# Longer runs from HBM, block turns on VectorE, and a down projection split by output columns in a streaming expert kernel

## The chip, the cores and the metric

The kernel runs on one core of one Trainium2 chip, the other cores idle. The metric is the device time of one execution in microseconds. Engines are named as in the profile: PE is TensorE (PEld its weight loads), DVE is VectorE, ACT is ScalarE, POOL is GpSimd, SP is SyncE, which here only issues DMAs.

## What is computed

One layer on 256 tokens of width 1024, all in float32: a mixer (input projection, two short convolutions, a gated recurrence, output projection), a layer norm, then an expert layer, and a second layer norm. The time goes to the expert layer. Cut to what matters:

```python
logits = xt @ w_router + b_router                 # 256 tokens, 32 experts
top_v, top_e = lax.top_k(logits, 4)
gates = softmax(top_v)
def expert(xb, e):                                # tokens routed to e
    h = xb @ w_gu[e] + b_gu[e]                    # 1024 -> 2048
    h_glu = min(h[:, :1024], 7); h_lin = clip(h[:, 1024:], -7, 7)
    act = h_glu * sigmoid(1.702 * h_glu) * (h_lin + 1)
    return act @ w_dn[e] + b_dn[e]                # 1024 -> 1024
ffn = sum over the 4 experts of a token of gate * expert(x)
x = layer_norm(DEEPNORM_ALPHA * x + ffn)
```

Each expert has 8.39 MB of gate-up weights and 4.19 MB of down weights, and all 32 are read once. On these inputs the reference routes between 21 and 44 tokens to an expert. The kernel handles them in blocks of 32 token slots: 18 experts take one block and 14 take two, 46 blocks in all. By expert number from 0, two blocks belong to 3, 4, 7 to 11, 14 to 16, 21, 24, 26 and 29.

## The kernel before, in words

**Loading.** SP issues all weight loads in one fixed order, on one queue. `gu_buf` holds two experts' gate-up weights, by the parity of the expert, each in four chunks of 2 MB (`GC` = 4, two slices `k` of 128 input rows each). `dn_buf` holds one expert's down weights in two halves of 2 MB (`DC` = 2). In the streaming loop (L270 to L274) the order is: down of expert e, then gate-up of expert e+1. A gate-up chunk may be overwritten when the last block of the expert two before has used it (`gu_used`), a down half when the last block of the expert before has used it (`dn_used`). Partition p of a gate-up chunk holds rows p and 128+p of the chunk's 256 rows, so one partition's part is two runs of 8 KB; of a down half it is four runs of 4 KB. One exception in the order stands at the start: the second down half of expert 2 (L266) and the load of `b_dn` (L268) come before the gate-up weights of expert 3.

**One block on PE** (`expert_block`, L790). PE multiplies 32 token slots by weights 256 or 512 columns at a time, and puts four such products side by side in the array, one in each group of 32 array columns, writing 32 of the 128 PSUM partitions each. Every float32 matmul is two instructions. In order: the gate-up product into bank `HB` (L797), its bias by a one-hot product (L807), the gather of the next block's 32 tokens (L757, `gather`), the first half of the sum of the *previous* block's results into the token accumulators (`combine(0)`, L767), two 128x128 transposes of the activation (`turn(TB, lin)`, L763), `combine(1)`, transposes of the gated one-hot (`gated`, which becomes `back`, the matrix that sends slots to tokens) and of the gathered rows, and the down product (L834). The down product leaves, for a group j of 256 hidden units, a partial sum over all 1024 output columns on partitions 32j to 32j+31, in banks `Y0` and `Y1`; `combine` adds the four partial sums in the same 128-row product that sends slots to tokens. The accumulators fill banks 0 to 3 for the whole expert loop.

**The other engines in a block.** DVE makes `gated` and the next `onehot`, clamps, multiplies to the activation `lin` (L619 to L625), copies the turned activation out of PSUM (L628) and half of the result (L630). ACT does the sigmoid, copies `rows`, `back`, `rows_t` and the other half of the result (L386 to L394).

**Start and end.** `start_sum` (L710) puts the scaled input in the accumulators, between the router's steps. At the end PE does one last `combine`, and DVE computes the layer norm's statistics of each 512-column piece as soon as it is summed (L634), then normalises, and SP stores.

## Time and profile before

| | us |
|---|---|
| median of 3 runs (lowest, highest) | 1086.83 (1084.99, 1091.21) |
| span of the profiled execution | 1088.8 |
| PE busy, share of the span | 946.0 (87%) |
| PE weight loads | 367.4 (34%) |
| DVE busy | 249.4 (23%) |
| ACT busy | 112.2 (10%) |
| moved by DMA | 422.59 MB, mean 388 GB/s over the span |
| chain that ended last, by engine | PE 63%, DMA 26%, SP's queue 8% |

A busy share is a mean over stages with different limits: the stage before about 125 us is the mixer and the router, then comes the expert stream, and from about 1063 us the end. The profiled execution lies 2.0 us above the median of the runs. Stretches are given in microseconds from the start of the span. The landing of a transfer is read from the instruction that waited for it.

### The profile page before, as it was taken

The numbers are of one execution on the slowest core, as the hardware profiler recorded it, in microseconds if no ns is written. First come the engines' busy times: TensorE is split into PE (matmuls) and PEld (weight loads), VectorE is DVE, ScalarE is ACT, GpSimd is POOL, SyncE is SP. The second block draws the span as 40 slices with busy tenths as digits, with TensorE's granted clock in tenths as the row PEclk, the third lists the DMA queues.
The fourth block names the chain that finished last, engine by engine and source line by source line (L and its number), as shares of the span: only waits on it lengthen the run. The fifth ranks groups of instructions, "written<-read, shape, count | busy, mean of one in ns | idle before, by whom it ended". The sixth has DMA issues, their size and how long they took to land.

```text
span 1088.8 us, 16845 instructions
## 1 busy us (share of the span) xinstructions
PE 946.0 (87%) x6739; PEld 367.4 (34%) x6740; DVE 249.4 (23%) x661; ACT 112.2 (10%) x265; POOL 7.3 (1%) x26
## 2 busy tenths in 40 slices
PE   8999998999669999997699997666977897976986
PEld 7884432333113333331133332211322332321322
DVE  3552511222112222221022221111211221211214
ACT  1300210111001111110011110000100110100100
POOL 1000000000000000000000000000000000000000
PEclk9999999999979999998899998888998998987998
DMA  9978689999999999999999999999999999999995
GB/s 328 410 281 337 252 353 396 418 388 372 417 418 388 381 416 372 376 372 417 419 406 417 380 373 417 417 417 419 418 419 418 417 412 417 392 417 417 396 420 224
DMA packets 80135, 422.59 MB, mean 388 GB/s; under 512 B 5804, under 2 KB 8152, under 8 KB 47352
## 3 DMA queue, kind: packets, MB, share of 16 engines
q1 hardware_dynamic: 77848, 421.96, 95.8%
q10 hardware_dynamic: 2272, 0.41, 0.2%
q8 instruction: 12, 0.20, 0.1%
q14 instruction: 3, 0.02, 0.0%
HBM read 421.30 MB, written 1.05 MB: 388 GB/s over the span
## 4 chain that ended last, share of the span: by engine, by line
PE 63%; DMA 26%; SPq 8%; issue 1%; DVE 1%; ACT 0%; DVEq 0%
DMA gu_buf<-in_w_gate_up_dram 21%; PE ps L797 20%; PE ps L767 12%; PE ps L834 12%; SPq L249 7%; PE ps L667 6%; DMA dn_buf<-in_w_down_dram 5%; PE ps L807 3%; PE ps L757 3%; PE ps L695 3%; PE ps L763 2%; SPq L254 1%; DMA gu_buf<-in_w_in_dram 0%; PE ps L682 0%; SPq L243 0%
## 5 line engine op out<-in xcount | busy, mean ns | idle before, releaser
L797 PE MATMUL ps<-gu_buf,rows_t 128*32 128x512 f32 x2944 | 379.5, 659 | 127.4 <-DMA gu_buf<-in_w_gate_up_dram 125.4
L797 PEld LDWEIGHTS ps<-gu_buf,rows_t 128*32 128x32 f32 x2944 | 95.3, 116 | 394.6 <-issue 202.7
L767 PE MATMUL ps<-mix,back 128*128 128x512 f32 x376 | 181.5, 606 | 0.0
L834 PE MATMUL ps<-dn_buf,act_t 128*32 128x512 f32 x1456 | 166.3, 595 | 1.3 <-DMA dn_buf<-in_w_down_dram 1.3
L619 DVE TENSOR_SCALAR glu<-ps 128x256 f32<-128x256 f32 x46 | 19.5, 425 | 404.2 <-PE ps L807 404.2
L630 DVE COPY mix<-ps 128x512 f32<-128x512 f32 x46 | 31.8, 692 | 247.2 <-PE ps L834 247.2
L767 PEld LDWEIGHTS ps<-mix,back 128*128 128x128 f32 x376 | 64.0, 190 | 65.2 <-issue 64.4
L386 ACT ACTIVATE sig<-glu 128x256 f32<-128x256 f32 x46 | 19.1, 416 | 576.5 <-DVE glu L619 576.5
L834 PEld LDWEIGHTS ps<-dn_buf,act_t 128*32 128x32 f32 x1456 | 42.4, 109 | 91.8 <-issue 73.9
L667 PE MATMUL ps<-turned,gu_buf 128*128 128x256 f32 x320 | 69.6, 379 | 1.3 <-DMA gu_buf<-in_w_in_dram 1.3
L667 PEld LDWEIGHTS ps<-turned,gu_buf 128*128 128x128 f32 x320 | 60.6, 190 | 9.7 <-issue 1.5
L807 PE MATMUL ps<-turned,bias_sel 128*32 128x512 f32 x368 | 52.4, 633 | 0.0
L757 PE MATMUL ps<-xs,onehot 128*32 128x256 f32 x752 | 50.5, 382 | 0.0
L757 PEld LDWEIGHTS ps<-xs,onehot 128*32 128x32 f32 x752 | 25.3, 112 | 38.7 <-issue 30.3
L394 ACT COPY mix<-ps 128x512 f32<-128x512 f32 x46 | 27.0, 586 | 108.4 <-PE ps L834 108.4
L390 ACT COPY back<-ps 128x256 f32<-128x256 f32 x46 | 17.1, 373 | 168.7 <-PE ps L763 168.7
L614 DVE TENSOR_SCALAR gated<-onehot,gates 128x128 f32<-128x128 f32 x92 | 22.2, 283 | 53.2 <-issue 53.2
L628 DVE COPY act_t<-ps 128x256 f32<-128x256 f32 x46 | 19.5, 425 | 53.5 <-PE ps L763 53.5
L605 DVE TENSOR_SCALAR onehot<-slot_iota,block_base,places 128x128 f32<-128x128 f32 x92 | 27.7, 344 | 7.2 <-DVE gated L614 7.2
L695 PE MATMUL ps<-gu_buf,mix 128*128 128x512 f32 x64 | 27.6, 592 | 0.0
L807 PEld LDWEIGHTS ps<-turned,bias_sel 128*32 128x32 f32 x368 | 13.9, 125 | 35.4 <-issue 35.4
L763 PEld LDWEIGHTS ps<-ident,gated 128*128 128x128 f32 x92 | 13.0, 142 | 24.2 <-issue 24.2
(173 smaller groups left out, 346.4 us busy)
## 6 DMA issues: line engine op xcount, KB each, us to landing
gu_buf<-in_w_gate_up_dram SPq DMA_DIRECT2D x128, 2048.0 KB, 24.1
dn_buf<-in_w_down_dram SPq DMA_DIRECT2D x63, 2048.0 KB, 16.3
gu_buf<-in_w_in_dram SPq DMA_DIRECT2D x4, 2048.0 KB, 17.1
gu_buf<-in_w_out_dram SPq DMA_DIRECT2D x2, 2048.0 KB, 14.4
gu_buf<-in_w_in_dram SPq DMA_DIRECT2D x2, 1024.0 KB, 6.6
xs<-in_x_dram SPq DMA_DIRECT2D x2, 512.0 KB, 3.6
late<-in_ln_g_dram SPq DMA_DIRECT2D x2, 512.0 KB, 21.6
late<-in_ln_b_dram SPq DMA_DIRECT2D x2, 512.0 KB, 18.3
```

The costliest lines, as they stand in the source:

```text
L249: sp.dma_start(gu_buf[:, b, GK * c:GK * (c + 1), :], gu_src[bass.ds(e, 1)].rearrange("o p k n -> p (o k) n")[:, GK * c:GK * (c + 1), :]).t ...
L394: nc.scalar.copy(y_sb[:, 0:512], ps[:, Y0, :]).then_inc(S["y0_sb"], 1)
L605: ins = V.tensor_scalar(onehot[:, h], slot_iota[:], base, column(h), ALU.add, ALU.is_equal)
L630: V.tensor_copy(y_sb[:, 512:D], ps[:, Y1, :]).then_inc(S["y1_sb"], 1)
L667: ins = T.matmul(half(banks[c // 2], c % 2), w_piece[:, piece_slot[i], k, P * c:P * (c + 1)], turned[:, k, :], start=(k == 0), stop=(k == ...
L695: return T.matmul(ps[:, 2 * h + c, :], mix[:, k, P * h:P * (h + 1)], w_out_v[:, n, 512 * c:512 * c + 512], start=(n == 0), stop=(n == KT - 1))
L757: ins = T.matmul(ps[SLOTS * j:SLOTS * (j + 1), Y0, 0:QF], onehot[:, h, 0, :], xs[:, h, QF * j:QF * (j + 1)], start=(h == 0), stop=(h == TH ...
L763: ins = T.transpose(ps[:, bank, P * b:P * (b + 1)], src[:, P * b:P * (b + 1)], ident[:])
L767: return [T.matmul(ps[:, 2 * h + c, :], back[:, P * h:P * (h + 1)], y_sb[:, 512 * c:512 * c + 512], start=False, stop=False, skip_group_ch ...
L797: ins = T.matmul(ps[SLOTS * j:SLOTS * (j + 1), HB, :], rows_t[:, k % 2, SLOTS * (k // 2):SLOTS * (k // 2 + 1)], gu_buf[:, b, k, :].rearran ...
L807: ins = T.matmul(ps[SLOTS * j:SLOTS * (j + 1), HB, :], bias_sel[:, j, :], b_gu, start=False, stop=True)
L834: ins = T.matmul(ps[SLOTS * j:SLOTS * (j + 1), Y0 + c, :], act_t[:, m, SLOTS * j:SLOTS * (j + 1)], weights[j][:, 512 * c:512 * c + 512], s ...
```

## The change

- **Runs.** Partition p now holds rows 8p to 8p+7 of a weight matrix. A chunk of gate-up or a half of down is one run of 16 KB per partition, and one partition's runs lie 64 KB (gate-up) or 32 KB (down) from the next one's. What is loaded, its chunks and their order stay, but `b_dn` is now loaded in four pieces before the expert loop.
- **Turns.** With rows 8p+q on partition p, the 32x32 block transpose of DVE gives the stationary operand that slice q needs. `rows_t` and `act_t` are each made by one DVE instruction that reads the source with a step of 8 elements; PE's transposes of `lin` and `rows`, and four copies (three on ACT, one on DVE; one of them L630), go.
- **Down by output columns.** Group j now computes output columns 256j to 256j+255 over all 1024 hidden units: 32 matmuls of 256 columns in place of 16 of 512, into half of one bank. `combine` is four products per token half, each of 32 rows (the slots of one group) by 256 columns, each with its own group of array rows and its own accumulator bank j. Both halves run in one place, after the gather; the gate-weighted `b_down` goes the same way.
- **Bias first.** The bias product opens the accumulation in `HB` in place of closing it, so the last gate-up chunk releases the result.
- **Start and end.** `start_sum` moves into the first expert block, in the place of its `combine`. The end has eight statistics of 256 columns, all after the last sum.

```diff
-        gu_src = w_gate_up[0].rearrange("e (k p) n -> e p k n", p=P)
-        dn_src = w_down[0].rearrange("e (j m p) n -> e m p j n", p=P, m=DC)
+        gu_src = w_gate_up[0].rearrange("e (p k) n -> e p (k n)", p=P)
+        dn_src = w_down[0].rearrange("e (p q) n -> e p (q n)", p=P)
...
+            for j in range(GROUPS):
+                sp.dma_start(b_dn[E * j:E * (j + 1), :], b_down[0][:, QF * j:QF * (j + 1)]).then_inc(S["bdn_in"], 16)
             sp.wait_ge(S["bounds_ok"], 1)
...
-            sp.dma_start(b_dn, b_down[0]).then_inc(S["bdn_in"], 16)
...
                 nc.scalar.activation(sig[:], glu[:], ACT.Sigmoid, scale=SWIGLU_ALPHA).then_inc(S["sig_ok"], 1)
-                act.wait_ge(S["rows_ps"], now)
-                nc.scalar.copy(rows[:], half(Y0, 0)).then_inc(S["rows_sb"], 1)
                 act.wait_ge(S["back_ps"], now)
-                nc.scalar.copy(back[:], half(Y1, 0)).then_inc(S["back_sb"], 1)
-                act.wait_ge(S["rows_t_ps"], now)
-                nc.scalar.copy(rows_t[:], half(HB, 0).rearrange("p (b s) -> p b s", b=2)).then_inc(S["rows_t_ok"], 1)
-                act.wait_ge(S["y0_ps"], now)
-                nc.scalar.copy(y_sb[:, 0:512], ps[:, Y0, :]).then_inc(S["y0_sb"], 1)
+                nc.scalar.copy(back[:], half(TB, 0)).then_inc(S["back_sb"], 1)
+                act.wait_ge(S["y_ps"], now)
+                nc.scalar.copy(y_sb, half(YB, 0)).then_inc(S["y_sb"], 1)
...
+            def in_blocks(v):
+                return v.rearrange("p (a q) -> p q a", q=KT)
...
+            dve.wait_ge(S["rows0_ps"], 1)
+            V.transpose(rows_t[:], in_blocks(half(Y0, 0))).then_inc(S["rows_t_ok"], 1)
...
+                dve.wait_ge(S["act_ok"], now)
+                V.transpose(act_t[:], in_blocks(lin[:])).then_inc(S["act_t_sb"], 1)
+                dve.wait_ge(S["rows_ps"], now)
+                V.transpose(rows_t[:], in_blocks(half(RB, 0))).then_inc(S["rows_t_ok"], 1)
...
-                dve.wait_ge(S["y_ps"], now)
-                V.tensor_copy(y_sb[:, 512:D], ps[:, Y1, :]).then_inc(S["y1_sb"], 1)
+                dve.wait_ge(S["back_ps"], now)
...
-            def combine(c):
-                return [T.matmul(ps[:, 2 * h + c, :], back[:, P * h:P * (h + 1)], y_sb[:, 512 * c:512 * c + 512],
-                                 start=False, stop=False, skip_group_check=True) for h in range(TH)]
+            def combine(h, stationary, moving):
+                for j in range(GROUPS):
+                    ins = T.matmul(ps[:, j, QF * h:QF * (h + 1)], stationary[SLOTS * j:SLOTS * (j + 1), P * h:P * (h + 1)],
+                                   moving[SLOTS * j:SLOTS * (j + 1), :], start=False, stop=False, skip_group_check=True)
+                return ins
...
+                pe.wait_ge(S["sel_bias"], now)
+                for j in range(GROUPS):
+                    T.matmul(ps[SLOTS * j:SLOTS * (j + 1), HB, :], bias_sel[:, j, :], b_gu, start=True, stop=False)
                 pe.wait_ge(S["rows_t_ok"], now)
...
-                                           start=(k == 0), stop=False)
+                                           start=False, stop=(k == KT - 1))
...
-                            ins = T.matmul(ps[SLOTS * j:SLOTS * (j + 1), Y0 + c, :], act_t[:, m, SLOTS * j:SLOTS * (j + 1)],
-                                           weights[j][:, 512 * c:512 * c + 512], start=(m == 0), stop=(m == DC - 1))
+                            ins = T.matmul(ps[SLOTS * j:SLOTS * (j + 1), YB, 0:QF], act_t[:, DK * m + q, :],
+                                           weights[q][:, QF * j:QF * (j + 1)],
+                                           start=(m == 0 and q == 0), stop=(m == DC - 1 and q == DK - 1))
```

On PE, the body of one block in the loop over pairs of experts, before (x4 and the like count matmuls of a run; `ps` is PSUM, `mix` there holds the result copied out of PSUM, `turned` the bias table):

```order
L797 MATMUL ps<-gu_buf,rows_t 32x512 x32
L807 MATMUL ps<-turned,bias_sel 32x512 x4
L757 MATMUL ps<-xs,onehot 32x256 x8
L767 MATMUL ps<-mix,back 128x512 x2
L763 MATMUL ps<-ident,lin 128x128 x2
L767 MATMUL ps<-mix,back 128x512 x2
L763 MATMUL ps<-ident,gated 128x128 x2
L763 MATMUL ps<-ident,rows 128x128 x2
```

and of the changed kernel, the same body with its down product:

```order
L809 MATMUL ps<-turned,bias_sel 32x512 x4
L812 ISA
L815 MATMUL ps<-gu_buf,rows_t 32x512 x32
L773 MATMUL ps<-xs,onehot 32x256 x8
L785 MATMUL ps<-mix,back 128x256 x8
L779 MATMUL ps<-ident,gated 128x128 x2
L840 REGISTER_ALU
L843 MATMUL ps<-dn_buf,act_t 32x256 x16
L840 REGISTER_ALU
L843 MATMUL ps<-dn_buf,act_t 32x256 x16
```

The bias moved ahead of the gate-up product, the two halves of `combine` stand together as eight short products, and between the gate-up product and the down product four transposes are gone.

On DVE, the part of the block's body after the gate-up product, before:

```order
L619 TENSOR_SCALAR glu<-ps 128x256
L620 TENSOR_SCALAR lin<-ps 128x256
L622 SCALAR_TENSOR_TENSOR lin<-lin,glu 128x256
L625 TENSOR_TENSOR lin<-lin,sig 128x256
L626 REGISTER_ALU
L626 COPY bias_sel<-ident 128x128
L628 COPY act_t<-ps 128x256
L630 COPY mix<-ps 128x512
```

and in the changed kernel:

```order
L635 TENSOR_SCALAR glu<-ps 128x256
L636 TENSOR_SCALAR lin<-ps 128x256
L638 SCALAR_TENSOR_TENSOR lin<-lin,glu 128x256
L641 TENSOR_TENSOR lin<-lin,sig 128x256
L643 STREAM_TRANSPOSE act_t<-lin 128x256
L645 STREAM_TRANSPOSE rows_t<-ps 128x256
L646 REGISTER_ALU
L646 COPY bias_sel<-ident 128x128
```

The turn of the activation follows the last multiply directly, without PE between them, and the copy of the result has left DVE.

## Rows read from the trace of the kernel before

**Rows 1.** The page: GB/s in 40 slices, and the gate-up group.
```profile
GB/s 328 410 281 337 252 353 396 418 388 372 417 418 388 381 416 372 376 372 417 419 406 417 380 373 417 417 417 419 418 419 418 417 412 417 392 417 417 396 420 224
...
L797 PE MATMUL ps<-gu_buf,rows_t 128*32 128x512 f32 x2944 | 379.5, 659 | 127.4 <-DMA gu_buf<-in_w_gate_up_dram 125.4
```
**Rows 2.** Windows: stretch, length, busy of five engines, PE clock, DMA share, GB/s.
```profile
271.00:316.00 45.00, 27.25 (x186) 7.05 (x182) 5.72 (x16) 2.01 (x5) 0.00 (x0) 0.88 1.01 418
411.00:444.00 33.00, 33.00 (x276) 11.91 (x272) 7.89 (x22) 4.02 (x10) 0.00 (x0) 1.00 0.94 381
```
**Rows 3.** Chain of waits, one PE-bound block: start, us, engine and line.
```profile
205.34 6.87 PE ps L797 x64
212.21 0.86 PE ps L807 x8
213.07 0.86 PE ps L757 x16
213.93 1.91 PE ps L767 x4
215.84 0.22 PE ps L763 x2
216.06 1.72 PE ps L767 x4
217.78 0.44 PE ps L763 x4
218.22 3.57 PE ps L834 x32
```
**Rows 4.** Timeline of PE: start, duration, group, and the wait before it.
```profile
505.21 1.92 PE L797 MATMUL ps<-gu_buf,rows_t 128*32 128x512 f32 x16 [1.66 <-DMA gu_buf<-in_w_gate_up_dram]
510.19 3.45 PE L797 MATMUL ps<-gu_buf,rows_t 128*32 128x512 f32 x16 [3.06 <-DMA gu_buf<-in_w_gate_up_dram]
...
514.33 1.04 PE L757 MATMUL ps<-xs,onehot 128*32 128x256 f32 x16
...
525.39 1.06 PE L797 MATMUL ps<-gu_buf,rows_t 128*32 128x512 f32 x8 [2.16 <-DMA gu_buf<-in_w_gate_up_dram]
```
**Rows 5.** Windows, the mixer's stretch with runs of 2 KB.
```profile
15.00:24.00 9.00, 9.00 (x44) 7.89 (x43) 4.80 (x29) 1.80 (x4) 0.00 (x0) 1.00 1.10 363
```
**Rows 6.** Groups by line: duration per instruction after the bar.
```profile
L390 ACT COPY back<-ps 128x256 f32<-128x256 f32 x46 | 17.1, 373 | 168.7 <-PE ps L763 168.7
...
L873 PE MATMUL ps<-mix,turned 32*128 32x512 f32 x8 | 3.7, 600 | 0.0
```
**Rows 7.** Timeline of DVE in one block.
```profile
514.58 0.42 DVE L619 TENSOR_SCALAR glu<-ps 128x256 f32<-128x256 f32 x1 [16.33 <-PE ps L807]
...
515.83 0.42 DVE L625 TENSOR_TENSOR lin<-lin,sig 128x256 f32<-128x256 f32 x1
...
517.54 0.42 DVE L628 COPY act_t<-ps 128x256 f32<-128x256 f32 x1 [1.14 <-PE ps L763]
```
**Rows 8.** The page, DMA issues: count, KB each, median us from issue to landing.
```profile
gu_buf<-in_w_gate_up_dram SPq DMA_DIRECT2D x128, 2048.0 KB, 24.1
dn_buf<-in_w_down_dram SPq DMA_DIRECT2D x63, 2048.0 KB, 16.3
...
xs<-in_x_dram SPq DMA_DIRECT2D x2, 512.0 KB, 3.6
```
**Rows 9.** Timeline: SP's first streamed loads.
```profile
126.96 6.84 SPq L249 DMA_DIRECT2D gu_buf<-in_w_gate_up_dram  x4
```
**Rows 10.** Timeline: the last block and the end.
```profile
1062.93 3.57 PE L797 MATMUL ps<-gu_buf,rows_t 128*32 128x512 f32 x16 [3.06 <-DMA gu_buf<-in_w_gate_up_dram]
1066.32 1.03 PE L807 MATMUL ps<-turned,bias_sel 128*32 128x512 f32 x8
...
1078.89 0.70 DVE L498 BATCH_NORM_STATS2 small<-ps 128x6 f32<-128x512 f32 x1 [0.16 <-PE ps L767]
...
1084.92 1.40 DVE L515 SCALAR_TENSOR_TENSOR xs<-ps,small,late 128x512 f32<-128x512 f32 x2
```

More of the change, by code:

```diff
@@ L786, in turn_gates, with expert_block @@
                 for h in range(TH):
-                    ins = T.transpose(ps[0:E, TB, P * h:P * (h + 1)], gates[:, h, :], ident[:])
+                    for j in range(GROUPS):
+                        ins = T.matmul(ps[E * j:E * (j + 1), TB, P * h:P * (h + 1)], gates[:, h, :], ident[:], start=True, stop=True)
                 ins.then_inc(S["gates_t_ps"], 1)
-            def expert_block(now, after, b, loads, down, first=False):
+            def expert_block(prior, now, b, loads, down, first=False):
+                pe.wait_ge(S["sel_bias"], now)
+                for j in range(GROUPS):
+                    T.matmul(ps[SLOTS * j:SLOTS * (j + 1), HB, :], bias_sel[:, j, :], b_gu, start=True, stop=False)
                 pe.wait_ge(S["rows_t_ok"], now)
@@ L848, in expert @@
                 with pe.Fori(first, end) as g:
-                    expert_block(g + 1, g + 2, b, loads, down)
+                    expert_block(g, g + 1, b, loads, down)
             down_0 = [down_at(m, 16) for m in range(DC)]
-            expert_block(1, 2, 0, 16, down_0, first=True)
+            expert_block(0, 1, 0, 16, down_0, first=True)
             pe.wait_ge(S["bounds_ok"], 1)
@@ L867, in _ @@
                 pair_of_experts(pair)
-            pe.wait_ge(S["bdn_in"], 16)
+            pe.wait_ge(S["bdn_in"], 16 * GROUPS)
             pe.wait_ge(S["gates_t_ok"], 1)
             for h in range(TH):
-                for c in range(2):
-                    T.matmul(ps[:, 2 * h + c, :], gates_t[:, P * h:P * (h + 1)], b_dn[:, 512 * c:512 * c + 512],
-                             start=False, stop=False, skip_group_check=True)
+                combine(h, gates_t, b_dn)
             with pe.Fori(E // 2 - 1, E // 2) as pair:
```

175 lines of the change are left out of this document (80 added, 95 removed).

## Prediction

> **What bounds the kernel now.** I read the page's GB/s line first. It has a ceiling: from the seventh slice on it stands at 416 to 420 in 19 of 33 slices and dips to between 372 and 412 in the others [rows 1]. The windows say what the two kinds are. From 271 to 316 us PE is busy 27 of 45 us and waits, and 418 GB/s arrive; from 411 to 444 PE is busy throughout and only 381 arrive [rows 2]. So the stream has two regimes: where experts have one block, the transfers bind, and where two-block experts follow each other, PE does. An expert is 12.58 MB, 30.1 us at 418 GB/s; the chain of waits gives a block 6.87+0.86+0.86+1.91+0.22+1.72+0.44+3.57 = 16.45 us of PE without a gap [rows 3], so two blocks take 32.9 us. SP's loads are released by PE's use, so each such expert leaves the queue dry for about 2.8 us. The page counts 2944 gate-up matmul instructions, 64 to a block, 46 blocks [rows 1].
>
> How much is lost so? In the timeline the third and fourth gate-up chunks of one expert land at 505.21 and 510.19, 4.98 us apart; the next landing PE waited for, 525.39, comes after two down halves and a chunk, 15.20 us, so a down half takes 5.11 us [rows 4]. Of the 128 gate-up chunks 8 are loaded before the stream, of the 63 down halves 2 before it and 2 after the last chunk [rows 8]: 120 and 59 lie between the first issue at 126.96 [rows 9] and the last landing at 1062.93 [rows 10]. With a full queue they take 120 x 4.98 + 59 x 5.11 = 899 us; they take 936. After about 2 us of latency (a 512 KB load takes 3.6, of which 1.3 is data [rows 8]) some **35 us** are queue idle. PE's slack in the one-block stretches is worth nothing.
>
> **The change, part by part.**
>
> *PE's block.* Bias, gate-up product and gather keep their shapes: 0.86 + 6.87 + 0.86. The down product streams as many columns, 32 matmuls of 256 for 16 of 512. Its shape (32 output rows, 256 columns) is the gather's, whose 8 matmuls take 0.86 in the chain [rows 3]; four times that is 3.4, and I keep 3.57. The transposes of `lin` and `rows` go, 0.22 each. `combine` was 1.91 + 1.72. Eight products of 32 rows by 256 columns now: no row shows four row groups at once. The nearest for a low bound is the gather, where four column groups share the array, 0.86 for the same count; the high bound is one after another: an instruction of 512 columns takes 1.72/4 = 0.43 in a stream [rows 3], and 16 of half the columns 3.4 (few rows make none shorter: those of the `b_down` product on 32 rows are listed at 0.60 like the others [rows 6]). I take 1.1, nearer the gather, since each row group has its own accumulator bank.
>
> The Trainium skill (TensorE: Matmul & The Clock Gate, Part 3: Packing small matmuls) gives four row tiles 3.07 times the speed of one after another; no run so far shows it here. By that the combine is 3.4/3.07 = 1.1 us.
>
> *The turn takes the lead.* PE cannot start the down product before `act_t`. In one block the gather starts at 514.33 [rows 4], the clamp on DVE at 514.58, and the last multiply ends at 516.25 [rows 7]. A block turn of 128x256 is not in the trace. Its low bound is nothing saved or lost against the copy out of PSUM, 0.42 [rows 7]; as a high one I take the four copies' worth, 1.7, for a read with a step of 8. I choose 0.42, the row of the same size and type. Then `act_t` is ready 1.67 + 0.03 + 0.42 after the clamp starts, 2.4 after the gather, and PE starts the down product at 2.5. PE's own work there is 0.86 + 1.1 + 0.22 = 2.2, so it waits 0.3: the combine is hidden as long as it costs less than 1.4. Behind the wait on PE stands only the down product. The turn of the rows comes next on DVE, 0.42 more, and is needed only when the next gate-up product starts, 4 us later; the one-hot copy behind it too is early. ACT loses three copies, DVE one; neither engine was late. **A block is 0.86 + 6.87 + 2.5 + 3.57 = 13.8 us**, two are 27.6.
>
> *Runs.* A down half in runs of 4 KB is 32 runs per DMA engine, a gate-up chunk in runs of 8 KB is 16, for the same bytes: 5.11 - 4.98 = 0.13 us for 16 runs more, 8 to 9 ns each [rows 4]. Runs of 2 KB arrived at only 363 GB/s [rows 5], in the same sense. With 8 runs of 16 KB, both kinds take 4.98 - 8 x 0.009 = **4.90 us** (428 GB/s), an estimate from those landings. An expert is 29.4 us, above two blocks at 27.6: PE is never late in the stream. The bounds: no gain over 8 KB runs, 4.98 (or over today's mean, 5.02); the layout's wide steps could cost, see the rivals.
>
> *Does the queue stay full?* For a two-block expert whose last chunk lands at t, its down halves land by t + 9.8 and the next expert's chunks by t + 29.4. The first block ends at about t + 11.6, the second at t + 25.4, so the next down half is issued at t + 23.6, 5.8 us before the queue is dry. At the start, the second down half of expert 2 no longer waits for a slow pair of blocks: PE comes to it some 4 us earlier, and 1 or 2 us of idle may stay there. The first block's `combine` becomes `start_sum`, 8 full products, 3.4 us as by the high bound above, which is what the old combine cost there. The bias ahead of the first gate-up product delays its first chunk, and SP's first issue, by about 0.3 us; the four `b_dn` loads fall in a stretch in which SP waits for the block bounds.
>
> *The end.* Before, from the last chunk's landing 15.96 us pass to the last sum (1078.89), and 9.9 from there to the end of the span [rows 10]. Now: 3.4 us for that chunk as before, when the bias started 3.39 after the landing (16 instructions take 3.45 and 3.57 after waits of 3.06, and 1.92 after one of 1.66) [rows 4, 10]; the bias, 0.86, is ahead; `act_t` 2.5 later; half of the down product, then a wait for the last down half, which lands at 9.8 (two transfers); 1.8 for the other half, 0.25 and a copy of 0.37 like ACT's of the same size [rows 6], 1.1 for the sums: 13.3, so 2.6 less. But all statistics now follow the last sum: eight of 256 columns at about 0.42 are 3.4, for two of 0.70 that followed it before [rows 10]: 2.0 more. The end is 25.9 - 0.6 = 25.3 us.
>
> **Sum.** 127.3 + 2 + 179 x 4.90 = 1006.4 for the last chunk's landing, + 25.3 = 1031.7 of span. The span of the profiled execution was 2.0 above the median of the runs, so **1029.7 us**. Of the 57 us, 35 are idle of the queue that goes, 22 the longer runs, less 0.3, and 0.6 comes at the end.
>
> **Rivals.**
>
> *A: the longer runs bring nothing.* The queue is always full but moves at today's mean of 5.02 (the DMA engines' share of 1.01 to 1.02 in full stretches [rows 2] says they have no gaps to give back). 129.3 + 899 + 25.3 - 2 = 1052 us. For it: no 16 KB run is in the trace. Against: two run lengths differ by a steady cost for each run.
>
> *B: PE still binds.* The four row groups run one after another, or the turn takes over 1.3 us. Serial: 0.86 + 3.4 + 0.22 + 0.1, a block of 15.9, two are 31.8 against 29.4: 2.4 of idle per two-block expert where it was 2.8, about 30 us in all: 1060. It decides from a block of 14.7 us. Against: column groups do run together [rows 3].
>
> *C: the wide steps between runs slow HBM, and the kernel is slower than before.* [...] The point from which the change loses is (1088.8 - 25.3 - 129.3)/179 = 5.22 us a transfer, 402 GB/s: 4% below today's rate in full stretches is enough. At 380 GB/s (5.52) the time is 1141. For it: nothing in this trace has such steps. Against: nothing either, beyond that the old layout had steps of 1 MB between the runs of one partition, at 418.
>
> The Trainium skill (DMA: Bandwidth & Descriptors, Latency and other measured facts) has a rule that speaks for C: tiles of 16 KB rows lose rate at large power-of-two pitches, from 2 MB on to 164 of 214 GB/s, while 512 KB still gave 207. The pitch here is 64 KB, so by its figures at most a few per cent are lost; no row here shows it.
>
> **How the numbers follow.** Forecast 0.62, A 0.17, B 0.11, C 0.08, and 0.02 for something in the first or last stage. The range must hold 8 in 10: forecast and A, with B's lower part. Below, runs at no cost each would be 4.98 - 16 x 0.009 = 4.84, 1019; above, B ends at 1060. So 1018 to 1060. About 0.5% is what a measurement of this kernel can tell from no change. Forecast, A and B are all faster by more; of C a third is near the old time. Faster 0.90, same 0.03, slower 0.07.
>
> **What would show it.** The GB/s line should be flat at 425 or more from 130 us to the end; A shows 418 flat, B dips, C lies flat and low. Landings should be 4.90 apart in both kinds. A block should last 13.8 in a two-block expert, PE's wait ahead of the down product should be for DVE's turn (0.3), with the turn at 0.42, and PE should wait for gate-up chunks in every expert. The first streamed load should be at about 127, the last chunk's landing at 1006. I am wrong in kind if the rate falls under 402 GB/s, or if PE shows no waits for chunks.

## The result, and the profile after

The changed kernel takes 1043.35 us, the median of 4 runs (1041.63 to 1045.26), against 1087.49 us (4 runs, 1084.99 to 1091.21) for the kernel before: a ratio of 0.9588, with a 95% interval of 0.9555 to 0.962. The forecast was 1029.7, so the time lies in its range, 13.6 us above the forecast itself. The profiled execution took 1045.26 us, with a span of 1043.3.

The page of the changed kernel: busy time and instructions of the engines, the granted clock and GB/s in 40 slices, and the groups of the two products (duration of one after the bar).

```profile
PE 834.9 (80%) x8423; PEld 361.2 (35%) x8424; DVE 242.2 (23%) x666; ACT 72.6 (7%) x171; POOL 6.1 (1%) x23
...
PEclk9999989899888999998899998877998998988987
...
GB/s 326 412 326 311 218 430 329 427 420 422 428 431 408 423 416 432 427 428 430 427 429 429 427 430 426 430 428 428 430 428 427 431 427 428 417 428 431 427 427 207
...
L815 PE MATMUL ps<-gu_buf,rows_t 128*32 128x512 f32 x2944 | 377.8, 658 | 117.5 <-DMA gu_buf<-in_w_gate_up_dram 117.5
...
L843 PE MATMUL ps<-dn_buf,act_t 128*32 128x256 f32 x2912 | 177.1, 389 | 50.6 <-DMA dn_buf<-in_w_down_dram 42.9
```

Beside [rows 1] the GB/s line is higher (427 to 432 where it was 416 to 420) and nearly flat, where it dipped in 14 of 33 slices. It is not quite flat: the seventh slice shows 329, the thirteenth 408, and a few others 416 to 423. Windows of the two stretches of [rows 2], which are 430 and 427 GB/s now instead of 418 and 381:

```profile
271.00:316.00 45.00, 29.76 (x280) 9.29 (x272) 7.29 (x22) 1.95 (x5) 0.00 (x0) 0.86 1.01 430
411.00:444.00 33.00, 31.43 (x384) 12.79 (x380) 7.55 (x22) 2.70 (x7) 0.00 (x0) 1.00 1.00 427
```

The timeline of PE in an expert with one block, and then a block of an expert with two, beside [rows 3, 4]; in brackets the wait before a group and what ended it:

```profile
507.54 1.92 PE L815 MATMUL ps<-gu_buf,rows_t 128*32 128x512 f32 x16 [2.98 <-DMA gu_buf<-in_w_gate_up_dram]
512.43 3.59 PE L815 MATMUL ps<-gu_buf,rows_t 128*32 128x512 f32 x16 [2.97 <-DMA gu_buf<-in_w_gate_up_dram]
517.34 1.92 PE L815 MATMUL ps<-gu_buf,rows_t 128*32 128x512 f32 x16 [1.32 <-DMA gu_buf<-in_w_gate_up_dram]
...
522.23 1.93 PE L843 MATMUL ps<-dn_buf,act_t 128*32 128x256 f32 x32 [0.66 <-DMA dn_buf<-in_w_down_dram]
527.13 1.93 PE L843 MATMUL ps<-dn_buf,act_t 128*32 128x256 f32 x32 [2.97 <-DMA dn_buf<-in_w_down_dram]
```

```profile
338.48 1.06 PE L809 MATMUL ps<-turned,bias_sel 128*32 128x512 f32 x8 [0.92 <-issue]
339.35 7.05 PE L815 MATMUL ps<-gu_buf,rows_t 128*32 128x512 f32 x64
346.22 1.05 PE L773 MATMUL ps<-xs,onehot 128*32 128x256 f32 x16
347.20 1.15 PE L785 MATMUL ps<-mix,back 32*128 32x256 f32 x16
348.28 0.44 PE L779 MATMUL ps<-ident,gated 128*128 128x128 f32 x2
348.96 3.42 PE L843 MATMUL ps<-dn_buf,act_t 128*32 128x256 f32 x57 [0.24 <-DVE act_t L643]
```

Chunks land 4.89 to 4.91 us apart and the two down halves 4.90, where it was 4.98 and 5.11. In the block of the second fence PE starts its down product 2.74 us after the gather. Of what had been `combine` and transposes (1.91, 0.22, 1.72, 0.44 in [rows 3]) there remain one `combine` of 1.08 us from start to start and the transposes of `gated`.

The last block and the end, beside [rows 10]:

```profile
1018.33 3.23 PE L815 MATMUL ps<-gu_buf,rows_t 128*32 128x512 f32 x16 [1.96 <-DMA gu_buf<-in_w_gate_up_dram]
...
1024.05 1.93 PE L843 MATMUL ps<-dn_buf,act_t 128*32 128x256 f32 x32 [0.18 <-DVE act_t L643]
1028.12 1.93 PE L843 MATMUL ps<-dn_buf,act_t 128*32 128x256 f32 x32 [2.13 <-DMA dn_buf<-in_w_down_dram]
1030.54 1.15 PE L785 MATMUL ps<-mix,back 32*128 32x256 f32 x16 [0.49 <-ACT mix L401]
```

The last chunk lands at 1018.33 instead of 1062.93, 44.6 us earlier, and the span ends 25.0 us later, where it was 25.9. So all but 1 us of the 45.5 us of span is gained in the stream. The sum of the prediction put that landing at 1006.4. The first streamed load is issued at 127.23 as it said (127.3), so the 11.9 us are lost in between, and the page says where to look first: the seventh slice. PE and windows of the DMA there:

```profile
137.66 3.42 PE L843 MATMUL ps<-dn_buf,act_t 128*32 128x256 f32 x60
146.30 1.93 PE L809 MATMUL ps<-turned,bias_sel 128*32 128x512 f32 x8 [5.22 <-issue]
148.00 8.35 PE L815 MATMUL ps<-gu_buf,rows_t 128*32 128x512 f32 x64
```

```profile
156.00:159.00 3.00, 2.82 (x42) 1.45 (x38) 2.47 (x6) 0.72 (x2) 0.00 (x0) 1.00 0.69 289
159.00:162.00 3.00, 3.00 (x60) 1.80 (x56) 1.31 (x6) 0.07 (x1) 0.00 (x0) 1.00 0.03 11
162.00:165.00 3.00, 2.35 (x32) 0.69 (x27) 0.00 (x0) 0.37 (x1) 0.00 (x0) 1.00 0.51 147
```

Between the only block of expert 0 and the first of expert 1, PE stands still for 5.22 us with nothing to wait for ("issue"). After that its bias product runs at half speed (1.93 instead of 1.07). SP is behind that block: it waits to load the second down half of expert 2 and cannot go on to the chunks of expert 3, and for some 5 us next to nothing is moved.

### The profile page after: what moved, and what is told of

The parts are those of the page before. It is cut to its first block, busy times and chain, and to the rows that moved or that the text cites. A ratio compares the mean times of both kernels' runs of the same rounds, so it can differ in the third digit from the quotient of the medians.

```text
span 1043.3 us, 20077 instructions
## 1 busy us (share of the span) xinstructions
PE 834.9 (80%) x8423; PEld 361.2 (35%) x8424; DVE 242.2 (23%) x666; ACT 72.6 (7%) x171; POOL 6.1 (1%) x23
## 4 chain that ended last, share of the span: by engine, by line
DMA 51%; PE 40%; DVE 6%; issue 2%; SPq 0%; ACT 0%; DVEq 0%; POOL 0%; POOLq 0%
DMA dn_buf<-in_w_down_dram 51%; PE ps L815 14%; PE ps L843 13%; PE ps L683 7%; PE ps L711 3%; PE ps L809 2%; DVE act_t L643 1%; DVE lin L641 1%; DVE lin L638 1%; DVE glu L635 1%; DVE lin L636 1%; PE ps L666 0%; PE ps L698 0%; PE ps L730 0%; PE ps L671 0%
## 5 line engine op out<-in xcount | busy, mean ns | idle before, releaser
L843 PE MATMUL ps<-dn_buf,act_t 128*32 128x256 f32 x2912 | 177.1, 389 | 50.6 <-DMA dn_buf<-in_w_down_dram 42.9
L843 PEld LDWEIGHTS ps<-dn_buf,act_t 128*32 128x32 f32 x2912 | 90.1, 111 | 123.5 <-DMA dn_buf<-in_w_down_dram 56.9
L809 PE MATMUL ps<-turned,bias_sel 128*32 128x512 f32 x368 | 54.7, 668 | 22.4 <-issue 22.4
L773 PE MATMUL ps<-xs,onehot 128*32 128x256 f32 x752 | 53.3, 404 | 0.0
L785 PE MATMUL ps<-mix,back 32*128 32x256 f32 x736 | 52.7, 400 | 0.5 <-ACT mix L401 0.5
L785 PEld LDWEIGHTS ps<-mix,back 32*128 32x128 f32 x736 | 33.2, 184 | 21.3 <-issue 19.3
L630 DVE TENSOR_SCALAR gated<-onehot,gates 128x128 f32<-128x128 f32 x92 | 22.2, 284 | 66.9 <-issue 66.9
L401 ACT COPY mix<-ps 128x256 f32<-128x256 f32 x46 | 17.1, 372 | 213.2 <-PE ps L843 213.2
L643 DVE STREAM_TRANSPOSE act_t<-lin 128x256 f32<-128x256 f32 x46 | 29.7, 645 | 1.6
L711 PE MATMUL ps<-gu_buf,mix 128*128 128x512 f32 x64 | 27.6, 592 | 0.0
L809 PEld LDWEIGHTS ps<-turned,bias_sel 128*32 128x32 f32 x368 | 9.6, 115 | 41.0 <-issue 39.0
L779 PE MATMUL ps<-ident,gated 128*128 128x128 f32 x92 | 20.1, 300 | 0.0
L641 DVE TENSOR_TENSOR lin<-lin,sig 128x256 f32<-128x256 f32 x46 | 19.6, 425 | 1.6
## 6 DMA issues: line engine op xcount, KB each, us to landing
late<-in_ln_g_dram SPq DMA_DIRECT2D x2, 512.0 KB, 23.5
```

The costliest lines, as they stand in the source:

```text
L630: ins = V.tensor_scalar(gated[:, h, :], onehot[:, h].rearrange("p j s -> p (j s)"), gates[:, h, bass.ds(e, 1)], None, ALU.mult)
L641: V.tensor_tensor(lin[:], lin[:], sig[:], ALU.mult).then_inc(S["act_ok"], 1)
L643: V.transpose(act_t[:], in_blocks(lin[:])).then_inc(S["act_t_sb"], 1)
L711: return T.matmul(ps[:, 2 * h + c, :], mix[:, k, P * h:P * (h + 1)], w_out_v[:, n, 512 * c:512 * c + 512], start=(n == 0), stop=(n == KT - 1))
L773: ins = T.matmul(ps[SLOTS * j:SLOTS * (j + 1), Y0, 0:QF], onehot[:, h, 0, :], xs[:, h, QF * j:QF * (j + 1)], start=(h == 0), stop=(h == TH ...
L785: ins = T.matmul(ps[:, j, QF * h:QF * (h + 1)], stationary[SLOTS * j:SLOTS * (j + 1), P * h:P * (h + 1)], moving[SLOTS * j:SLOTS * (j + 1) ...
```

## Experiments

### The two halves of the change apart

`before_long` is the kernel before with the new layout of the weights in HBM read (runs of 16 KB). `after_short` is the changed kernel with the old runs, 8 KB for gate-up and 4 KB for down. In both the weights are multiplied with the rows in another pairing; the work is the same.

```diff
# before_long, against the kernel before
-        gu_src = w_gate_up[0].rearrange("e (k p) n -> e p k n", p=P)
-        dn_src = w_down[0].rearrange("e (j m p) n -> e m p j n", p=P, m=DC)
+        gu_src = w_gate_up[0].rearrange("e (p k) n -> e p (k n)", p=P)
+        dn_src = w_down[0].rearrange("e (p q) n -> e p (q n)", p=P)
# after_short, against the changed kernel
-        gu_src = w_gate_up[0].rearrange("e (p k) n -> e p (k n)", p=P)
-        dn_src = w_down[0].rearrange("e (p q) n -> e p (q n)", p=P)
+        gu_src = w_gate_up[0].rearrange("e (c k p) n -> e c p k n", p=P, c=GC)
+        dn_src = w_down[0].rearrange("e (j m p) n -> e m p j n", p=P, m=DC)
```

> The kernel before with the loads of the changed one: one run of 16 KB per partition, the block on PE as it was. The rows of the weights reach the wrong slices, so the output is not the reference's; every instruction and byte is. Theory (transfers of 4.90 us, but the pairs of blocks of 32.9 us on PE stay as they are): only the 18 one-block experts can gain their 0.73 us, about 13 us, 1075, with the PE-bound stretches still at 381 GB/s. Rival (the rate gives its 22 us wherever it acts, since the queue is what ends last): 1066. If long runs bring nothing without the other parts: 1088.

> The changed kernel with the old run lengths, two runs of 8 KB for a gate-up chunk and four of 4 KB for a down half; output not the reference's, since the rows of the weights reach the wrong slices. Theory: transfers of 4.98 and 5.11 again, 22 us more, less some idle that longer transfers cover (up to 5 us): 1060 to 1065. Rival on the 5.2 us for which PE stood still after its first block (an instruction fetch held up by long runs on the same DMA engines): that stall shrinks to the 1.4 of the kernel before and the time is 4 us lower still; if the jump causes it, it stays at 5.

Measured: `before_long` 1073.78 us (1072.2 to 1075.17), ratio 0.9866 (0.9843 to 0.9889); `after_short` 1064.37 us (1063.44 to 1064.41), ratio 0.9784 (0.9763 to 0.9805). The GB/s lines of the two:

```profile
GB/s 326 415 293 342 224 385 387 427 384 372 430 429 400 382 420 371 372 371 430 429 430 427 374 373 430 427 429 429 407 430 429 429 410 429 417 430 430 385 430 218
```

```profile
GB/s 326 409 310 309 236 416 332 418 415 416 417 417 420 419 418 417 417 418 417 417 418 419 418 418 417 418 417 417 418 419 419 417 417 417 416 418 416 419 418 225
```

The first has the new ceiling (427 to 430) and the old dips (371 to 387): where PE binds, longer runs bring nothing. The second has the old ceiling (415 to 420) and no dips but the one in the seventh slice. The layout alone saves 14.1 us and the PE side alone 23.5; together 44.1 to 44.5, so 7 us come only when both are there: a faster stream is worth more once PE no longer binds. In `after_short` the stop of PE is still there, 5.57 us long, so it does not come from the layout.

### What about the runs is it: their length or their distance

The prediction's rival C made the distance between the runs of neighbouring partitions the danger. `after_close` reads runs of 16 KB that lie side by side; `after_short_wide` reads the old run lengths at distances of 64 and 32 KB. The pairing of weights and rows is another in both, the work the same.

```diff
# after_close
-        gu_src = w_gate_up[0].rearrange("e (p k) n -> e p (k n)", p=P)
+        gu_src = w_gate_up[0].rearrange("e (c p k) n -> e c p (k n)", p=P, c=GC)
# after_short_wide
+        gu_src = w_gate_up[0].rearrange("e (p k c) n -> e c p k n", p=P, c=GC)
```

> The changed kernel with runs of 16 KB that lie next to each other: partition p of a 2 MB transfer takes the p-th 16 KB of one contiguous 2 MB, in place of runs 64 KB (32 KB for down) apart; output not the reference's, since the rows of the weights reach the wrong slices. Theory (only the length of a run counts): landings 4.90 apart as in the changed kernel, 1043. Rival C of the prediction (wide steps cost something): faster landings and over 5 us less; 4.85 a transfer would be 1034.

> The changed kernel with runs of 8 KB and 4 KB, but with the partitions as far apart as in it (64 KB and 32 KB); output not the reference's, for the same reason. Theory: as the run with short runs in the old places, 1064, transfers of 4.98 and 5.11. Rival (wide steps cost, and long runs hide it): slower than 1064 by over 5 us.

Measured: `after_close` 1043.57 us (1040.56 to 1046.08), 0.9571 (0.9538 to 0.9605), landings 4.88 to 4.90 apart (500.72, 505.61, 510.51, 515.39); `after_short_wide` 1064.59 us (1064.0 to 1067.46), 0.9781 (0.9748 to 0.9814), landings 4.97 and 5.12. Each is the time of its partner with the other distance, so of the two only the length of a run counts here, at these distances, and C is false.

### Where 12 us of the stream went

`after_noif` leaves out PE's loop for further blocks of expert 0, which has only one block with these inputs; it is thus no kernel for all inputs. `after_order` keeps everything and lets SP issue the first two chunks of expert 3 ahead of the second down half of expert 2.

```diff
# after_noif
             pe.wait_ge(S["bounds_ok"], 1)
-            end = pe.value_load(bounds[0:1, 1:2], min_val=1, max_val=MAXB)
-            with pe.If(end > 1):
-                with pe.Fori(1, end) as g:
-                    expert_block(g, g + 1, 0, 16, down_0)
# after_order
-            stream_dn_chunk(2, 1, blocks_before(2))
-            stream_gu(3, 1)
+            used = blocks_before(2)
+            for c in range(GC):
+                sp.wait_ge(gu_used[c], used)
+                sp.dma_start(gu_chunk(1, c), gu_src[3][:, GRUN * c:GRUN * (c + 1)]).then_inc(gu_in[1][c], 16)
+                if c == 1:
+                    stream_dn_chunk(2, 1, used)
```

> The changed kernel without the loop for further blocks of expert 0, which has one block on these inputs (the general case is left out). Theory (the jump over that loop's code makes PE fetch instructions, 5.2 us, and with it comes a dry queue at 158 to 163 us): PE goes on at about 142, the dry spell nearly goes, and the time is 5 us lower, 1038. Rival (the fetch comes at that place anyway, since the next expert's code is new too): within 1 us of the changed kernel, 1043.

> The changed kernel; only SP's order at the start differs: the first two gate-up chunks of expert 3 are issued before the second down half of expert 2, which waits for PE. Theory (the dry spell at 158 to 163 us costs the end its full length, since the queue is full later): the spell goes although PE stalls as before, 5 to 6 us less, 1038. Rival (the idle is given back later because blocks of a pair, at 14.4 us and more, bind somewhere): less than 2 us gained, 1042.

Measured: `after_noif` 1036.24 us (1035.48 to 1039.16), 0.9535 (0.951 to 0.9559); `after_order` 1038.28 us (1035.23 to 1039.19), 0.9535 (0.951 to 0.956). PE at the same place in `after_noif`, and the windows of `after_order` where nothing was moved before:

```profile
141.29 1.07 PE L809 MATMUL ps<-turned,bias_sel 128*32 128x512 f32 x8 [0.24 <-issue]
```

```profile
156.00:159.00 3.00, 3.00 (x44) 1.42 (x34) 1.96 (x5) 0.42 (x1) 0.00 (x0) 1.00 1.01 421
159.00:162.00 3.00, 2.82 (x54) 1.62 (x56) 1.57 (x7) 0.37 (x1) 0.00 (x0) 1.00 1.02 437
162.00:165.00 3.00, 2.38 (x36) 0.84 (x32) 0.25 (x1) 0.37 (x1) 0.00 (x0) 1.00 0.99 421
```

Without the code of the loop the stop is gone (0.24), so it comes from passing over that code. In `after_order` the stop is there (5.35), but the queue has chunks to move meanwhile. In both, the last chunk lands at 1008.5 (1008.54 and 1008.49), 9.8 us earlier, and the GB/s line is nearly flat to the end. Most of these 9.8 of the 11.9 us were time in which the queue was empty: by windows of 3 us the changed kernel misses an estimated 8.4 us of full-rate transfer more than `after_order`. But the dry spell at the start is only about half of them; that the later dips are gone too is no work of these two edits (see the next section). And of the 9.8 us `after_order` keeps only 6.1 in the span (1037.2): its last down half lands 11.2 us behind the last chunk instead of 9.8, and PE runs it at half clock (3.64 us) and the last sum partly so (1.82), so its span ends 28.7 us after that chunk, where it is 25.0 in the changed kernel and in `after_noif`. The kernel before has a smaller stop near the same place, 0.22 and 1.43 us; why the new one is longer isn't settled. (PE executes 8423 matrix instructions instead of 6739, so a block's code has grown; no run varied its length.)

### The dips after that: how long a block may be

Two edits of the block. `after_nobias` leaves the bias product out; `after_turn2` turns `act_t` a second time.

```diff
# after_nobias
-                pe.wait_ge(S["sel_bias"], now)
-                for j in range(GROUPS):
-                    T.matmul(ps[SLOTS * j:SLOTS * (j + 1), HB, :], bias_sel[:, j, :], b_gu, start=True, stop=False)
# after_turn2
+                V.transpose(act_t[:], in_blocks(lin[:])).then_inc(S["act_t0"], 1)
+                dve.wait_ge(S["act_t0"], now)
                 V.transpose(act_t[:], in_blocks(lin[:])).then_inc(S["act_t_sb"], 1)
```

> The changed kernel without the bias product of the gate-up result, 0.86 us of PE per block (the bias is left out, the output is not the reference's). Theory (beyond the dry spell at the start, blocks of a pair at 14.4 to 15.4 us are just late for the queue, some 5 us of idle in all): 3 to 5 us less, 1039. Rival (PE's length has no part left in the time, and all 12 us of idle hang on the start): within 1.5 us of 1043.

> The changed kernel with a second, useless block turn of the gated activations behind the first (DVE, 0.645 us and some 0.06 us of a link), so that every expert block is about 0.7 us longer between its gate/up product and its down product. Theory: the blocks of the experts with two blocks, at 13.9 to 14.5 us where an expert's transfers take 29.4, stand at the edge, and 0.7 us more puts two of them (29.4 to 30.2 with what comes around them) above it: the dips of the rate behind the doubled experts grow, 4 to 10 us in all, about 1050. Rival: the blocks have room to spare and only the last block, 0.7 us, is seen: 1044. Second rival: PE sets the pace in all blocks, 32 or more times 0.7: over 1060.

Measured: `after_nobias` 1041.05 us (1037.96 to 1043.18), 0.9551 (0.9515 to 0.9587); `after_turn2` 1044.68 us (1042.91 to 1045.71), 0.9595 (0.9559 to 0.963). The first is 2.3 us below the changed kernel, with overlapping runs, between its theory (3 to 5) and its rival (within 1.5); it decides nothing. The first theory on `after_turn2` fell in size (it gave 1050). PE's wait ahead of the down product grows from 0.25 to 0.92 us in each block. In the five doubled experts in a row (7 to 11) an expert then takes PE 29.8 to 30.3 us (first bias products at 365.35, 395.69, 425.50 and 455.79) against 29.4 of transfers; PE waits for no transfer between 318.09 and 475.96, and the landings slip by 1.2 us over that stretch. So there the blocks do stand just past the edge, but it costs some 1 us and not 4 to 10, and in its profile the last chunk lands at 1015.92, earlier than in the changed kernel's. The changed kernel's own dips are thus not set by the length of a block at full clock. What sets the largest of them shows in one place of two traces, an expert with two blocks, where the first block waits for the second down half and the second block follows at once. First the changed kernel, then `after_turn2`:

```profile
318.76 3.64 PE L843 MATMUL ps<-dn_buf,act_t 128*32 128x256 f32 x32 [2.97 <-DMA dn_buf<-in_w_down_dram]
322.17 1.93 PE L809 MATMUL ps<-turned,bias_sel 128*32 128x512 f32 x8
323.88 7.45 PE L815 MATMUL ps<-gu_buf,rows_t 128*32 128x512 f32 x64
```

```profile
318.09 1.93 PE L845 MATMUL ps<-dn_buf,act_t 128*32 128x256 f32 x32 [2.70 <-DMA dn_buf<-in_w_down_dram]
319.84 1.04 PE L811 MATMUL ps<-turned,bias_sel 128*32 128x512 f32 x8
320.70 7.05 PE L817 MATMUL ps<-gu_buf,rows_t 128*32 128x512 f32 x64
```

After a wait of 2.97 us the changed kernel's PE ran its down half and the next bias product at half speed; after one of 2.70 the other ran at full. From the landing to the second block's gate-up product it takes 5.12 us in the one and 2.61 in the other, and 0.4 more is lost in that product. The queue of SP in each: the next expert's down halves are issued at 336.03 in the changed kernel and at 333.11 in `after_turn2`, although the latter's block is longer:

```profile
336.03 2.06 SPq L274 DMA_DIRECT2D dn_buf<-in_w_down_dram  x2
```

```profile
333.11 2.06 SPq L274 DMA_DIRECT2D dn_buf<-in_w_down_dram  x2
```

In the windows, 257 GB/s arrive from 336 to 339 us in the changed kernel and 426 in `after_turn2`. Which wait is followed by half clock differs from kernel to kernel. Near the end `after_close`, with the same instructions, runs the down half behind its wait of 2.97 us at half clock (3.64 us at 966.41); the next down halves are issued at 983.69, 27.1 us after the expert's last chunk has landed, and 254 GB/s arrive from 984 to 986. The changed kernel runs that down half at full clock (1.93 us at 967.84, after 2.96), issues after 24.1 us (982.19), and 410 arrive in the same window. This reading rests on the traces; no run held the clock up through the stream.

It does not cover everything. At 4.90 us a transfer, the changed kernel's landings slip by 0.6 us between 200.64 and 264.91, by 2.7 between 318.76 and 380.27, and by 1.5 between 967.84 and 998.76. In the first two stretches the down half behind the wait ran partly or wholly at half clock (2.55 and 3.64 us). In the third it ran at full clock and the windows show no dip; what delayed that landing is open.

### The order of the bias product

`after_biaslast` puts the bias product behind the gate-up product, as it was before the change.

```diff
-                pe.wait_ge(S["sel_bias"], now)
-                for j in range(GROUPS):
-                    T.matmul(ps[SLOTS * j:SLOTS * (j + 1), HB, :], bias_sel[:, j, :], b_gu, start=True, stop=False)
                 pe.wait_ge(S["rows_t_ok"], now)
...
+                pe.wait_ge(S["sel_bias"], now)
+                for j in range(GROUPS):
+                    ins = T.matmul(ps[SLOTS * j:SLOTS * (j + 1), HB, :], bias_sel[:, j, :], b_gu, start=False, stop=True)
+                ins.then_inc(S["h_ps"], 1)
```

> The changed kernel with the four bias products of a block behind its gate/up product instead of ahead of it; nothing else moves. The number of instructions is the same, so a block of a doubled expert takes PE as long as now. At the end of the program 0.9 to 1.7 us (the four products at full or half clock) come between the last gate/up chunk and the end: 1044 to 1045 by that, and the last landing stays near 1018. Rival: bias first, which on TensorE runs while a chunk lands, also shortens the start of every block after a transfer wait, so that moving it back costs at many blocks: 1050 or more. Rival in the other direction: no difference within 1 us, the products fit in beside waits at the end too.

Measured: 1040.11 us (1039.9 to 1041.06), 0.9552 (0.9517 to 0.9587). This was expected wrongly in size and sign: it is 3.2 us below the changed kernel's median, with no run in common (the intervals of the two ratios do overlap, 0.9587 and 0.9555). Its end:

```profile
1012.95 2.81 PE L812 MATMUL ps<-gu_buf,rows_t 128*32 128x512 f32 x16 [2.98 <-DMA gu_buf<-in_w_gate_up_dram]
1015.51 1.92 PE L822 MATMUL ps<-turned,bias_sel 128*32 128x512 f32 x8
...
1022.76 1.93 PE L845 MATMUL ps<-dn_buf,act_t 128*32 128x256 f32 x32 [0.92 <-DMA dn_buf<-in_w_down_dram]
```

The bias product now stands on the path behind the last chunk, and still the span ends 24.95 us after that landing (1037.9): PE waits for the last down half in either order, 0.92 us instead of 2.13. So bias first is worth nothing at the end. In the stream, bias last gives each chunk's buffer back 0.87 us earlier, and the GB/s line has no dip after the seventh slice, nor do its landings slip; whether the earlier return or the clock behind the waits is the reason, these runs don't tell apart.

### The four row groups

`after_serial` lets all eight products of `combine` read the same 32 partitions, one row group; it sums the first group's slots four times.

```diff
-                    ins = T.matmul(ps[:, j, QF * h:QF * (h + 1)], stationary[SLOTS * j:SLOTS * (j + 1), P * h:P * (h + 1)],
-                                   moving[SLOTS * j:SLOTS * (j + 1), :], start=False, stop=False, skip_group_check=True)
+                    ins = T.matmul(ps[:, j, QF * h:QF * (h + 1)], stationary[0:SLOTS, P * h:P * (h + 1)],
+                                   moving[0:SLOTS, :], start=False, stop=False, skip_group_check=True)
```

> The changed kernel with all eight products of the combine on the same 32 array rows, so that they cannot run side by side; the first group's slots are summed four times, so the output is not the reference's. Theory (four row groups share the array, 0.86 us for sixteen instructions, and in series they take 3.4): a block is 1.9 us longer, 16.3, a pair 32.6 against 29.4 of transfers, about the kernel before with long runs, 1074. Rival (the combine's cost is hidden behind VectorE's turn, or row groups never ran together): 1043 to 1050.

Measured: 1118.04 us (1108.52 to 1121.55), 1.0275 (1.0233 to 1.0317). Slower than the kernel before, and 44 us above what was expected. PE in one block, and windows beside it (the column before the DMA share is the granted clock):

```profile
413.65 4.49 PE L785 MATMUL ps<-mix,back 32*128 32x256 f32 x16
418.06 0.69 PE L779 MATMUL ps<-ident,gated 128*128 128x128 f32 x2
418.68 5.90 PE L843 MATMUL ps<-dn_buf,act_t 128*32 128x256 f32 x64
425.36 1.06 PE L809 MATMUL ps<-turned,bias_sel 128*32 128x512 f32 x8 [0.77 <-issue]
```

```profile
413.00:416.00 3.00, 3.00 (x27) 2.19 (x20) 2.61 (x7) 0.42 (x1) 0.00 (x0) 1.00 0.87 371
416.00:419.00 3.00, 3.00 (x13) 1.66 (x15) 0.00 (x0) 0.21 (x1) 0.00 (x0) 0.57 0.00 0
419.00:422.00 3.00, 3.00 (x32) 1.39 (x28) 1.09 (x4) 0.16 (x1) 0.00 (x0) 0.50 0.00 0
```

One after another, the products took 4.41 us up to the next group's start instead of 1.08. The first 2.35 us of them ran at a clock of 1.00, the rest at about 0.57, which makes an estimated 3.5 us at full clock, the high bound that the prediction used. What was not expected is the clock: it fell during this group without any wait before it and stayed at 0.50 through most of the down product, which took 5.90 instead of 3.66 us. The block lasts 20.4 us (404.95 to 425.36). So the four row groups do run together, at about a third of the price in series: 3.2 times, by the estimate of 3.5 against 1.08. The Trainium skill (TensorE: Matmul & The Clock Gate, Part 3: Packing small matmuls) gives 3.07 times for four row tiles with 512 columns each; the trace, with 256 columns, agrees with it roughly.

### A version that is faster than both

`after_warm` is `after_order` with useless products on the identity, ten at a time, ahead of the second to fourth chunk and ahead of the second down half of the last expert alone, where PE waits about 3 us for a landing.

```diff
                 for c in range(GC):
+                    if c:
+                        keep_warm(RB, warm)
                     pe.wait_ge(gu_in[b][c], loads)
...
+                    if m:
+                        keep_warm(HB, warm)
```

> The changed kernel with SyncE's order around expert 3 (first two gate/up chunks of expert 3 ahead of the second down half of expert 2, as in after_order, 1038.3 us) and, in the last expert alone, ten useless 128x128 products (some 2.6 us) on TensorE ahead of the second, third and fourth gate/up chunk and ahead of the second down half, where it waits 3.0 to 3.3 us for a landing. Theory: with them the engine stays at the higher granted clock (1.0), the product on the last gate/up chunk takes about 1.9 us instead of 3.4, that of the last down half 1.9 instead of 3.6, the last combine 1.15 instead of 1.8; on the path that sets the end 2.4 us of that (the second down half waits for its landing anyway): 1035 to 1036. Rival: the useless products run over the landings and hold up the work by as much as they give: 1038 or above.

Measured: 1035.76 us (1035.63 to 1036.1), 0.9509 (0.9475 to 0.9544). The end of `after_order`, then that of `after_warm`:

```profile
1019.66 3.64 PE L846 MATMUL ps<-dn_buf,act_t 128*32 128x256 f32 x32 [3.34 <-DMA dn_buf<-in_w_down_dram]
1023.80 1.82 PE L788 MATMUL ps<-mix,back 32*128 32x256 f32 x16 [0.49 <-ACT mix L404]
```

```profile
1016.00 2.50 PE L669 MATMUL ps<-ident 128*128 128x128 f32 x20
1018.96 1.93 PE L850 MATMUL ps<-dn_buf,act_t 128*32 128x256 f32 x32 [0.46 <-DMA dn_buf<-in_w_down_dram]
1021.38 1.15 PE L788 MATMUL ps<-mix,back 32*128 32x256 f32 x16 [0.49 <-ACT mix L404]
```

From the landing of the last down half to the end of the span it is 17.5 us in the first (1037.2) and 15.1 in the second (1034.1): the 2.4 us that the clock had cost. It stands 2.5 us below `after_order` in the median, and its four runs lie within 0.5 us where those of `after_order` cover 4.0, the lowest of them 1035.23. That would fit a filling that makes the good case come every time, but only one execution of each is profiled, and that of `after_order` is its slowest. It is 7.6 us below the changed kernel, by the new order of the loads above all: in the changed kernel's profile the last down half (1.93 us) and the last sum (1.15) ran at full clock without any filling.

## Why the prediction was nearly right, and where it failed

**The two regimes** of [rows 2] were real: each half of the change, alone, moves one of them (`before_long`, `after_short`).

**The transfers.** 4.90 us for both kinds was forecast from the difference of two run lengths, and 4.89 to 4.91 was measured. Rival A (1052) is thereby out for the changed kernel, and rival C by `after_close`.

**The block.** Forecast 13.8 us: 0.86 + 6.87 + 2.5 + 3.57. Measured from start to start: 0.87 + 6.87 + 2.74 + 3.46 = 13.94, and then, behind an expert's last block, 0.41 or 0.92 us of "issue" ahead of the next expert's bias product, which the sum did not have (22.4 us over 29 places, the 5.2 among them). `combine` at 1.08 for a forecast of 1.1 was right, and so was the wait for the turn (7.7 us in 32 places, 0.24 each, for 0.3). The turn itself was mis-sized: 0.646 us instead of 0.42, since I took the row of a plain copy for an operation that the trace did not show; the turn out of PSUM took 0.41. It was not what cost the 13.6 us: as `after_turn2` shows, 0.7 us more in each block cost 1.3 us in all, which four runs hardly tell from nothing. Two blocks thus take 28.3 to 28.8 us and not 27.6, so the room below the 29.4 of the transfers is 0.6 to 1.1 us and not 1.8. The sign that PE waits for gate-up chunks in every expert did not hold either: between 318.76 and 473.27, in experts 7 to 11, it waits only for down halves, 0.2 to 0.9 us. Rival B's serial form would have been worse than it said (1118 measured for 1060), since it did not know of the clock.

These are the rows for the turns:

```profile
421.07 0.65 DVE L643 STREAM_TRANSPOSE act_t<-lin 128x256 f32<-128x256 f32 x1
421.65 0.41 DVE L645 STREAM_TRANSPOSE rows_t<-ps 128x256 f32<-128x256 f32 x1
```

**"Does the queue stay full?" is the step that failed, in the main.** It said that the idle of 35 us goes, but for 1 or 2 us at the start. The last chunk landed 9.8 us later than with the fullest queue of these runs. It failed in two places. At the start it looked at SP's order and at PE's pace, and not at PE's jump past a loop that isn't run, though the kernel before showed 1.65 us of "issue" there; the jump takes 5.2 us now, and the queue is dry for it (`after_nobias` and `after_biaslast`, which have this dry spell and hardly another, land their last chunk at 1013.91 and 1012.95, 4.5 to 5.4 us behind the full queue's 1008.5). And for a block behind a transfer wait it used durations at full clock: it had the down half issued at t + 23.6, where t is the landing of the expert's last chunk; in the case above t is 318.76 - 9.8 = 308.96 and the issue comes at t + 27.1. Of the 3.5 us, 1.6 are the down half at half clock, 1.3 the bias and gate-up products behind it, 0.2 the turn, and 0.3 lie between PE's use of the buffer and SP's issue. That leaves 2.3 us until the queue is dry, hardly more than the 2 us taken for the way to the first byte. Of the remaining 4.4 to 5.4 us of the changed kernel's 9.8, some 3.3 are such dips by the landings (0.6 and 2.7); the 1.5 between 967.84 and 998.76 are not explained.

**The base of the sum.** 127.3 + 2 + 179 x 4.90 = 1006.4 was 2.1 us too little even for a queue that never runs dry (1008.5). Small slips that `after_order` keeps (some 0.6 us between the landings at 194.82 and 259.13, 0.3 between 959.17 and 998.70) are part of it; the rest is not traced.

**The end.** 25.3 forecast, 25.0 measured, right also in its parts: the last down half lands 9.8 us after the last chunk, and the last sum starts 12.2 after it. That the bias is ahead did not matter for it, as `after_biaslast` showed.

**From span to time.** I took 2.0 us off the span because the span of the profiled execution before lay that much above the median. That was one run's chance: an execution takes about 2.0 us longer than its span (1045.26 around the changed kernel's 1043.3), so the execution profiled before lay some 4 us above its median and that of the changed kernel 1.9, with a span equal to the median. This step had no mechanism, and cost 2.0 us. So the miss is 9.8 + 2.1 - 0.3 + 2.0 = 13.6.

## What to carry to other kernels

When a stream is paced by one queue whose loads wait for the consumer, give the durations of the consumer at both clocks that it may have after its waits, and look at each place where it passes over code; then order the queue so that a load whose buffer is free isn't behind one whose buffer isn't (here 5 us for a few lines). Of a price that the trace doesn't show, ask first whether it is on the path: the turn was 50% off and cost nothing that the runs can tell. In this program, bound by transfers, filling the last waits of TensorE with useless products was worth 2.4 us against an execution whose end went at half clock, while in the changed kernel's profile the end was at full clock without it.

## What the runs showed of the hardware

- Passing over a loop's code that isn't run stopped TensorE for 4.9 to 5.9 us in ten kernels; without that code (`after_noif`) the gap is 0.24.
- A transfer of 2 MB takes 4.90 us in runs of 16 KB, 4.97 to 4.98 in runs of 8 KB and 5.11 to 5.12 in runs of 4 KB, whether the runs of neighbouring partitions lie side by side or 32 to 64 KB apart.
- A block turn of 128x256 fp32 on DVE takes 0.646 us from SBUF and 0.407 from PSUM (each 46 times, within 17 ns).
- Eight 32-row products of 256 columns take 1.08 us on four row groups and 4.41 on one; on one, the granted clock fell from 1.00 to 0.50 without a wait before it, and most of the down product behind it went at that clock.
- After a wait of 3.0 us the next group ran at full or at half speed (1.92 or 3.59 for the same 16 instructions, at 507.54 and 512.43); products on the identity in the waits of the last expert kept it at full in `after_warm`.
